# Bursts of identity matmuls ahead of fifteen waits of TensorE, in a two-block transformer kernel

## The reference, cut to what matters

```python
def first_block(x, mem, ...):
    proj = rmsnorm(h, norm_mix_pre) @ w_in
    y_conv = short_conv_mixer(bg, cg, xin, conv_w)
    y_att = nsa_mixer(q, kc, vc, ksl, vsl, kw, vw, ...)
    mixed = concatenate([rmsnorm(y_conv), rmsnorm(y_att)])
    h = h + rmsnorm(mixed @ w_out, norm_mix_post)
    hn = rmsnorm(h, norm_x_pre)
    px = softmax((hn @ w_q_x) @ kx.T * X_HEAD_DIM ** -0.5)
    h = h + rmsnorm((px @ vx) @ w_o_x, norm_x_post)
    hn = rmsnorm(h, norm_ffn_pre)
    g, up = split(hn @ w_gate_up)
    return h + rmsnorm((silu(g) * up) @ w_down, norm_ffn_post)

def hybrid_layer(x, mem, ...):
    z = rmsnorm_2(x, g_mix) @ w_in
    y = gates[0] * (h_m @ w_proj_mlstm) + gates[1] * (h_na @ w_proj_na) + gates[2] * (h_mem @ w_proj_mem)
    x = x + y @ w_out
    u = rmsnorm_2(x, g_ffn) @ w_up
    return x + square(relu(u)) @ w_down
```

## Time and profile before

| | us |
|---|---|
| three runs | 1708.65, 1711.47, 1715.67 |
| median | 1711.47 |
| the profiled execution | 1716.15 |
| its span, first to last instruction | 1714.4 |
| TensorE busy in it | 1660.4 (97%) |
| ScalarE, VectorE, GpSimd busy | 663.6, 616.3, 728.8 |
| mean granted TensorE clock | 0.985 |

### The profile page before, as it was taken

The page is one execution under the profiler, slowest core; times in us unless marked ns, Lnnn a source line. Parts: engine busy times, 40 slices in busy tenths (PEclk is TensorE's granted clock), DMA queues, the critical chain, the costliest instruction groups (busy, mean ns, idle before and its releaser), DMA issues. The chain is left out here.

```text
span 1714.4 us, 22737 instructions
## 1 busy us (share of the span) xinstructions
PE 1660.4 (97%) x8732; PEld 1330.9 (78%) x8732; DVE 616.3 (36%) x1160; ACT 663.6 (39%) x1009; POOL 728.8 (43%) x639
## 2 busy tenths in 40 slices
PE   9989899999899999999988999999999999999999
PEld 7767678787678888888877787767788888888887
DVE  5432765432232102111147544454556331213131
ACT  4223577454253233222234534343554442313140
POOL 5223334562144444454434544323445354444443
PEclk9989899999999999999999999999999999999999
DMA  5243201342032333343221224222254223232321
GB/s 179 75 147 85 72 26 51 126 147 72 25 99 74 123 99 85 92 147 95 86 88 55 99 96 147 77 77 85 75 191 165 99 75 99 98 99 98 99 98 49
DMA packets 152943, 166.06 MB, mean 97 GB/s; under 512 B 11959, under 2 KB 114434, under 8 KB 152835
## 3 DMA queue, kind: packets, MB, share of 16 engines
q1 hardware_dynamic: 145232, 151.20, 27.4%
q10 hardware_dynamic: 7602, 13.41, 2.2%
HBM read 155.68 MB, written 9.30 MB: 96 GB/s over the span
## 5 line engine op out<-in xcount | busy, mean ns | idle before, releaser
L805 POOL TENSOR_TENSOR w_low<-raw,w_high 128x512 fp32r<-128x512 f32 x501 | 661.0, 1350 | 867.5 <-ACT w_high L950 867.0
L950 ACT CAST w_high<-raw 128x2048 fp32r<-128x2048 f32 x127 | 239.4, 1885 | 236.7 <-PE bank L2293 223.6
L2298 PE MATMUL bank<-xT_high,w_high 128*128 128x512 f32 (+1 forms) x672 | 251.0, 378 | 0.0
L2299 PE MATMUL bank<-xT_low,w_high 128*128 128x512 f32 (+1 forms) x672 | 250.6, 377 | 0.0
L2288 PE MATMUL bank<-w_high,hid_low 128*128 128x512 f32 x432 | 170.0, 394 | 0.0
L2287 PE MATMUL bank<-w_high,hid_high 128*128 128x512 f32 x432 | 169.9, 393 | 0.0
L2302 PE MATMUL bank<-xT_high,w_low 128*128 128x512 f32 (+1 forms) x672 | 157.3, 376 | 1.8 <-POOL w_low L805 1.7
L2201 PE MATMUL bank<-xT_high,w_high 128*128 128x512 f32 (+1 forms) x360 | 152.2, 423 | 0.7 <-ACT qbuf L1308 0.4
L2299 PEld LDWEIGHTS bank<-xT_low,w_high 128*128 128x128 f32 x672 | 128.8, 192 | 22.3
L2298 PEld LDWEIGHTS bank<-xT_high,w_high 128*128 128x128 f32 x672 | 128.5, 191 | 22.3
L2203 PE MATMUL bank<-xT_high,w_low 128*128 128x512 f32 (+1 forms) x360 | 142.8, 397 | 0.0
(11 more groups left out here) (428 smaller groups left out, 2537.9 us busy)
## 6 DMA issues: line engine op xcount, KB each, us to landing
raw<-in_w_in SPq DMA_DIRECT2D x33, 1024.0 KB, 5.0
raw<-in_w_down SPq DMA_DIRECT2D x26, 1024.0 KB, 5.0
raw<-in_w_gate_up SPq DMA_DIRECT2D x44, 512.0 KB, 4.5
raw<-in_w_up SPq DMA_DIRECT2D x16, 1024.0 KB, 5.2
raw<-in_w_kv_x SPq DMA_DIRECT2D x8, 1024.0 KB, 5.3
raw<-in_w_out SPq DMA_DIRECT2D x8, 1024.0 KB, 5.0
gate_dram<-qbuf ACTq DMA_DIRECT2D x20, 256.0 KB, 2.0
sg<-gate_dram ACTq DMA_DIRECT2D x6, 768.0 KB, 5.1
```

Source lines behind the costliest of these rows:

```text
L805: ins = pool.tensor_tensor(low[:, cs], full[:, cs], high[:, cs], ALU.subtract)
L950: own.tell(act.copy(split_slot(c, wh), split_slot(c, raw)), wh_done)
L2298: pe.matmul(ps[:, t0:t1], ch[:, k, cs], xh[:, k, t0:t1], start=q == 0, stop=False)
L2299: pe.matmul(ps[:, t0:t1], ch[:, k, cs], xl[:, k, t0:t1], start=False, stop=False)
```

## The change

`keep_warm` takes the bank to write as a second argument and is called in fifteen more places, each just before a wait: 104 more identity matmuls in all. Where the bank might still be read, a wait for its reader stands ahead of the burst (`o_taken`, `s_taken`, `conv_rms`, `x_exp`). Nothing is taken away, and no other engine's program changes. The places and numbers: in `last_half` before `turn(phase, 0)` 4 (hx), 7 (hf) and 18 (h2); in `first_tiles` 9 (h2, at its start) and 7 (hf, after the second tile); 3 ahead of the wait for `cmp_kv_in` and 10 ahead of `kc_rot`; 7 and 6 in steps 8 and 9; 5 in step 10 and 5 in step 11; 8 before `low_all("att")`; 6, 3 and 6 at the end of the cross-attention.

```diff
+            def keep_warm(n, unused):
+                for _ in range(n):
+                    pe.matmul(unused[:, 0:P], ident[:, :], ident[:, :], start=True, stop=True)
...
+            WARM = {"hx": 4, "hf": 7, "h2": 18, "h4": 0}
...
             def last_half(c, xh, xl, phase):
...
                     if j == 1:
                         product(c[3], 0, xh, xl)
                     else:
+                        if j == 2:
+                            keep_warm(WARM[phase], SB[0])
                         turn(phase, j - 2)
                     product(c[3], j, xh, xl)
 
             def first_tiles(tiles, phase):
+                if phase == "h2":
+                    keep_warm(9, SB[0])
                 turned_ready(phase, 2)
                 for i, (c, k) in enumerate(tiles):
                     product(c, k, xTh, xTl, part=(0, S // 2))
+                    if phase == "hf" and i == 1:
+                        keep_warm(7, SB[0])
                     if i < 2:
                         turn(phase, 2 + i)
...
             turn_hidden(1)
+            keep_warm(3, bank[3])
             pe.wait_ge(cmp_kv_in, 2)
...
             mm.then_inc(cmp_kv, 1)
+            keep_warm(10, bank[3])
             pe.wait_ge(kc_rot, 1)
...
                         pe.wait_ge(s_exp, 2 * i + g + 1)
+                        if g == 1 and s in (8, 9):
+                            pe.wait_ge(o_taken, 1)
+                            keep_warm(15 - s, bank[2])
...
                 if s == SUM_STEP:
+                    pe.wait_ge(s_taken, 2 * s + 2)
+                    keep_warm(5, SB[0])
                     pe.wait_ge(conv_sq, 4)
...
                 if s == SUM_STEP + 1:
+                    pe.wait_ge(conv_rms, 1)
+                    keep_warm(5, bank[3])
                     pe.wait_ge(conv_inv, 1)
...
+            pe.wait_ge(s_taken, 4 * ST * PER_GROUP)
+            keep_warm(8, SB[0])
             low_all("att")
...
                     hd, qt = i // ST, i % ST
+                    if it == XH * ST:
+                        pe.wait_ge(x_exp, it - 1)
+                        keep_warm(6, SB[0])
                     pe.wait_ge(x_norm, i + 1)
...
                     hd = it // 4 - 1
+                    if hd == XH - 1:
+                        keep_warm(3, SB[0])
                     pe.wait_ge(x_pta, hd + 1)
...
+            keep_warm(6, SB[0])
             pe.wait_ge(x_lo, 8)
             by_token("ox", oxTh, oxTl, "hf", first=2)
```

More of the change, by code:

```diff
@@ L2335, in low_all @@
                 turned_ready(phase, ST if phase not in ("mem", "mem2") else MT)
-            def keep_warm(n):
-                for _ in range(n):
-                    pe.matmul(bank[3][:, 0:P], ident[:, :], ident[:, :], start=True, stop=True)
             pe.wait_ge(const_ready, 2)
-            keep_warm(2)
+            keep_warm(2, bank[3])
             pe.wait_ge(mix_in, 16)
@@ L2347, in _ @@
             mm.then_inc(vec_tr, 1)
-            keep_warm(5)
+            keep_warm(5, bank[3])
             turn("x", 0)
-            keep_warm(8)
+            keep_warm(8, bank[3])
             def vectors():
```

## The result

| | before | changed |
|---|---|---|
| runs, us | 1708.44, 1708.65, 1708.70, 1711.47, 1715.67 | 1699.77, 1699.89, 1700.88, 1702.02, 1702.47 |
| median, us | 1708.70 | 1700.88 |
| profiled execution, us | 1716.15 | 1702.47 |
| its span, us | 1714.4 | 1700.8 |
| mean granted clock | 0.985 | 0.999 |

The ratio of changed to before is 0.9940, with an interval of 0.9926 to 0.9954. The forecast was 1702.3 us with a range of 1697 to 1709, and faster by over 0.5% as the likeliest case. By the medians both are a gain of 8 us, 0.46% and 0.47%. The ratios on record, which have the intervals and are not the quotients of these medians, give 0.60% and 0.42%, on the two sides of the half per cent.

What follows compares the result with a forecast made beforehand. TensorE, busy 97% of the span, was taken as the bound, with time lost at half clock. Seven stretches gave 11.5 us, plus 2.3 for those without bursts: 1716.15 - 11.5 - 2.3 = 1702.3 us, range 1697 to 1709.

Steps and rivals of the forecast that it cites:

- 1242: Low-clock stretch at 1242 us in the neighbourhood attention, without a burst; worth 1.6 us in the profiled execution.
- The cost of a burst: Burst matmuls at 0.20 us each, 20.8 us for 104, fit in 31.2 us of TensorE waits; cost 0, bounds 0 to 2 us.
- The start as evidence: At the kernel's start the clock rises among only transposes and identity matmuls, so such matmuls count as work.
- The added waits: The waits for `o_taken`, `s_taken`, `conv_rms` and `x_exp` cost 0, each being passed earlier than the wait that follows it.
- 225: Low-clock stretch at 225 us, behind the wait for the diagonal; 1.2 us gained, between 0.5 and 1.6, VectorE nearly the bound.
- 501.5: Low-clock stretch at 501.5 us, in hf behind a wait for normalised rows; 1.0 us gained, between 0 and 1.6.
- 890.5: Low-clock stretch at 890.5 us, in h2's 5.10 us wait; worth 0, at most 1.8 us, as VectorE sets the pace.
- my signs of being wrong: Mean clock staying at 0.985, burst matmuls of 0.4 us, or clock up with new VectorE waits over 1 us behind those places.
- the two unaddressed stretches: Low-clock stretches without a burst, in h2 behind GpSimd's low weights and in neighbourhood attention; 4.7 us together, 2.3 counted as absent.
- (a): Rival: the gain is swallowed further on, where VectorE sets the time; about 1707 us, chance 0.16.
- (c): Rival: the clock falls as before because such matmuls do not count or are too short; 1711.5 us, chance 0.07.
- (b): Rival: bursts cost more than they give, starting at half clock with up to 0.50 us a matmul; about 1721 us, chance 0.07.

## Why the prediction was right, point by point

**What bounds the kernel.** Right. TensorE's list is the time, nine low stretches stood in the profiled execution, and eight are gone with the idle time filled rather than shortened. One of the eight, at 1242, had no burst ahead of it and was absent all the same.

**The cost of a burst.** The figure was right and its reading wrong. I took eight records of the earlier trace rows for four transposes, 0.20 us each. They are eight transposes of 0.10 us. A plain float32 matmul is two records of about that length, so the figure came out near the 0.22 us that it takes (36 records in 4.18 us with the tail), by luck, through two errors that cancel; the run with transposes brought it to light. The cost beyond the waits was 0, as forecast: the bursts fit at all fifteen places, with 0.15 us left at the tightest (the sum of squares). Step 9 is among them, where the wait had grown from 0.84 to 2.0 us, of which the burst fills 1.5. The run with doubled bursts shows what it costs if they don't, 8.9 us for 104 matmuls more.

**The start as evidence.** That the clock rises there was read from durations: ten records in 2.50 us, then sixteen in 2.88 with a dense matmul at 0.39 us behind them. The windows view gives 1.00 from the first microsecond on. What held for the bursts does not rest on it, for the runs with plain matmuls and with twice as many transposes show it directly.

**The added waits.** Right as far as it can be told: 0.9990 with the waits alone, interval 0.9977 to 1.0002.

**The worth of the stretches.** Six of the seven terms came within 0.2 us (the table above), 225 with 0.4 us lost again by 315, on the side that I had given for VectorE. 501.5: 1.0 forecast and 1.6 measured, the one term that was mis-sized. I had thought that a weight cast in ScalarE's queue would hold the last turn of hf; in the changed kernel that turn came 1.6 us earlier too, with 0.66 us of its wait left behind the burst, so the chain follows the product that starts it and nothing is swallowed. 890.5: 0 and 0, and the run without its burst confirms it. Only the place was wrong: I had named the wait at 905.77 as the one that takes it, and it is the turn before, which now waits 1.78 us. The fixed 7 us of VectorE's loop are 7.01. That wait is also one of my signs of being wrong, a new wait for VectorE of over 1 us with the clock up. It stands at the one place priced at 0, so the sum does not suffer; the sign was drawn too wide.

**From the profiled execution to the median.** The weakest step, and it held by its size. I counted half of the two unaddressed stretches, 2.3 us; the trace shows 1.7. As a way to the median it was too simple, and that the two agree is in part luck. The kernel before is usually 4 to 5 us shorter than either of its profiled executions, while the changed kernel's profiled execution lies within 1.6 us of its median. The stretches that come and go over the traces are 501.5 and 522 of the seven and the two others, 914.5 and 1242, so what an ordinary execution lacks may be taken from either. So the change is worth 13.6 us against the slowest pattern and 8 us in the median, and a forecast as a difference from the median of 1711.47 (9.2 us) was 1 us too high. The chance for faster by over 0.5% was put at 0.57, and the two measurements, 0.60% and 0.42%, lie on both sides of that line; by the medians both lie short of it.

**The rivals.** (a) did not happen: what was gained up to 530 is there at the end but for a few tenths. (c) is refuted by the windows; the part of it that was true is that shorter bursts hold the clock at fewer places. (b), bursts that begin at half clock, did not occur with bursts of full length. It did at step 9 in the three traces with shorter ones, where six records last 1.48 (transposes), 0.98 and 0.97 us and leave no wait behind them. The first of these cost some 0.3 us; what (b) would cost at all fifteen places was not tried, and the doubled bursts show its mechanism, work beyond the end of the wait, at full clock.

## What to carry to other kernels

When one engine's list is the time, list the low stretches of its clock beside its waits, and price each by following it to the next wait: half of its busy time where that wait belongs to the same engine's work, nothing where another engine's loop sets the pace. Fill a wait with work that nobody reads up to its end and no further. Here bursts of half the length ended 2.7 and 4.4 us later than full ones in the traces, and bursts of twice the length 8.9 us later, for a matmul beyond the wait costs its full length unless another engine sets the pace. Before a profiled execution is compared with a median, look at the spread of the times and at the mean clock of each execution, for the low stretches make one kernel into several of different length; a second trace alone did not help here, for it showed the slowest pattern again.

## What was not expected of the hardware

- A transpose of a 128x128 float32 tile is one record of about 0.1 us, a plain float32 matmul on the same tile two, 0.22 us together: 10 records in 1.26 us against 20 in 2.45.
- Transposes hold the clock when they fill the same time, at fourteen of fifteen places: 1703.1 us against 1702.7 on the same chip.
- The clock of the same kernel falls at other places in other executions: nine stretches at 1716.15 and 1715.96 us, five at 1707.71 us with the added waits alone, and its times spread over 9.4 us on one chip and 4.1 us on another. With nearly all stretches gone the spread is 2.7 and 3.8 us, the latter beside the 4.1.
